# Eight modulation slots of the first block moved from TensorE to VectorE, as sixteen half slots during the projections

## The reference

```python
mod = c @ ada_w[l] + ada_b[l]          # c: 1x1024, ada_w: 1024 x 6144, 24 MB
shift1, scale1, gate1, shift2, scale2, gate2 = jnp.split(mod, 6, axis=-1)
h = _modulate(_rmsnorm(x, norm1_g[l]), shift1, scale1)
z = h @ w_in[l]                        # 256x1024 @ 1024x2720: "the projections"
zu, zv, zr = jnp.split(z, [GMLP_WIDTH, 2 * GMLP_WIDTH], axis=-1)
y_a = _gmlp_mixer(zu, zv, ...)         # gelu, layer norm, mixing by ws, + bs
y_b = _rwkv7_mixer(zr, ...)            # token shift, low-rank gates, a recurrence over tokens
y = jnp.concatenate([y_a, y_b], axis=-1) @ w_out[l]
x = x + gate1[:, None, :] * y
h = _modulate(_rmsnorm(x, norm2_g[l]), shift2, scale2)
y = _hier_moe(h, ...)                  # router, then 32 experts, 6 MB of weights each
x = x + gate2[:, None, :] * y
```

## Times and profile before

| | us |
|---|---|
| median of three runs | 1554.64 |
| lowest, highest | 1552.86, 1556.13 |
| the profiled execution | 1563.66 |
| its span, first to last instruction | 1561.6 |

### The profile page before, as it was taken

One profiled execution on the slowest core, in us unless ns is written; L12 is line 12 of the kernel. 1 busy time (PEld: TensorE's weight loads), 2 busy tenths in 40 slices (PEclk: granted clock), 3 DMA queues, 4 the chain that ended last, 5 costly groups with the idle time before them and its releaser, 6 DMA issues.

```text
span 1561.6 us, 21530 instructions
## 1 busy us (share of the span) xinstructions
PE 1491.0 (95%) x8432; PEld 952.6 (61%) x8433; DVE 463.7 (30%) x835; ACT 233.8 (15%) x469; POOL 22.0 (1%) x69
## 2 busy tenths in 40 slices
PE   6999999999989999999899999999999999999998
PEld 3766775544445444444585657777768564777775
DVE  1355544411111111111453422111144472211112
ACT  1231002300000000000313430000031052100001
POOL 2000000000000000000000000000000000000000
PEclk9999999999999999999999999999999999999999
DMA  9665523899999999999999050444276933144420
GB/s 370 219 258 217 220 110 141 341 404 423 422 417 393 426 426 426 427 427 424 407 402 351 19 222 30 162 162 161 81 264 246 397 116 108 55 162 162 161 81 27
DMA packets 89962, 400.82 MB, mean 257 GB/s; under 512 B 7040, under 2 KB 12288, under 8 KB 63264
## 3 DMA queue, kind: packets, MB, share of 16 engines
q1 hardware_dynamic: 89888, 399.73, 64.6%
HBM read 398.66 MB, written 1.05 MB: 256 GB/s over the span
## 4 chain that ended last, share of the span: by engine, by line
PE 76%; DMA 9%; DVE 7%; issue 3%; DVEq 3%; ACT 1%; SPq 0%; ACTq 0%
PE psum L1358 20%; PE psum L1027 13%; PE psum L1371 10%; DMA ring<-in_moe_up 6%; PE psum L1173 4%; PE psum L637 4%; PE psum L1321 4%; PE psum L1015 2%; DMA arena<-in_w_mod 2%; PE psum L760 2%; PE psum L1206 2%; DMA ring<-in_ada_w 1%; PE psum L566 1%; PE psum L1191 1%; DVE arena L1903 1%
## 5 line engine op out<-in xcount | busy, mean ns | idle before, releaser
L1027 PE MATMUL psum<-ring,arena 128*64 128x256 f32 (+1 forms) x2240 | 306.0, 426 | 18.8 <-DMA ring<-in_moe_up 8.2
L1358 PE MATMUL psum<-arena,ring 128*128 128x256 f32 x1408 | 311.3, 379 | 0.3
L1358 PEld LDWEIGHTS psum<-arena,ring 128*128 128x128 f32 x1408 | 267.1, 190 | 54.3 <-issue 19.8
L1027 PEld LDWEIGHTS psum<-ring,arena 128*64 128x64 f32 x2240 | 162.8, 137 | 170.5 <-issue 77.1
L1371 PE MATMUL psum<-ring,arena 128*128 128x512 f32 x352 | 157.9, 592 | 0.0
L2052 DVE TENSOR_SCALAR arena<-psum,cols 128x256 f32<-128x256 f32 x44 | 23.9, 544 | 323.3 <-PE psum L1358 323.3
L1173 PE MATMUL psum<-arena,ring 128*128 128x256 f32 x512 | 112.2, 380 | 1.5 <-DVE arena L1461 1.5
L1371 PEld LDWEIGHTS psum<-ring,arena 128*128 128x128 f32 x352 | 66.9, 190 | 66.3 <-issue 63.6
L1173 PEld LDWEIGHTS psum<-arena,ring 128*128 128x128 f32 x512 | 96.8, 190 | 16.6 <-issue 3.6
L1816 DVE TENSOR_TENSOR arena<-psum,arena 128x256 f32<-128x256 f32 x32 | 13.6, 425 | 252.1 <-PE psum L1027 252.1
L2392 ACT ACTIVATE arena<-arena 128x256 f32<-128x256 f32 x44 | 18.3, 416 | 415.8 <-DVE arena L2058 415.8
(11 more groups left out here) (383 smaller groups left out, 1238.7 us busy)
## 6 DMA issues: line engine op xcount, KB each, us to landing
ring<-in_moe_gate SPq DMA_DIRECT2D x28, 2048.0 KB, 19.4
ring<-in_moe_up SPq DMA_DIRECT2D x28, 2048.0 KB, 17.8
ring<-in_moe_down SPq DMA_DIRECT2D x28, 2048.0 KB, 18.1
arena<-in_w_mod SPq DMA_DIRECT2D x32, 1024.0 KB, 10.0
ring<-in_ada_w SPq DMA_DIRECT2D x12, 2048.0 KB, 10.4
ring<-in_w_qkv SPq DMA_DIRECT2D x12, 2048.0 KB, 15.0
ring<-in_w_ffn_gate SPq DMA_DIRECT2D x10, 2048.0 KB, 8.0
ring<-in_w_ffn_up SPq DMA_DIRECT2D x10, 2048.0 KB, 12.6
```

The lines of the kernel that those rows point to most:

```text
L1027: ins = mm(bank[b][o, 0:n], lhsT, w[:, half * n:(half + 1) * n], start=first, stop=last, tile_position=(0, 64 * half))
L1358: last = mm(b[:, k * TOK:(k + 1) * TOK], sl[k][2][:, c, j * P:(j + 1) * P], hTd[:, c, :], start=(c == 0), stop=(c == DC - 1))
```

## The change

Slots 4 to 11 of `ada_w` leave TensorE. VectorE does each in two half slots of 128x2048: one multiplication by a column of `c`, added to a running sum (`scalar_tensor_tensor`). Eight half slots make a sum of 128x2048; TensorE then adds its 128 rows up with a vector of ones (`add_slots`, four products) into `part`, and the chain of copy, `flush` and `mod_columns` follows. There are two such sums: `first_sums[0]` in the arena where `bkT` is later, `first_sums[1]` in ring place 0.

On VectorE the sixteen half slots stand as 3 before `shifted(0)`, 1 after it, 2 after `shifted(1)`, 2 after `shifted(3)`, 3 before `shifted(5)`, 3 after the bonus (behind a `mod_columns`), 2 after the gelu's normalization.

On SyncE the loads move up between those of the projections. Ring places come from a table, `FIRST_SLOTS`, for the first 24 loads. A load into a place last held by one of VectorE's slots waits for `mod_step`, which counts half slots. `w_mod0` 2 and 3 are loaded ahead of `w_out`, not after it; the first expert matrix is load 24, as before.

On TensorE the `fill` calls of the Gram products and of level 0 stay and now do `w_mod0` 0 to 3; the other eight slots' worth of `fill` is gone, and two `flush` calls move to the projections and behind the transposes.

```diff
+FIRST_SLOTS = (0, 1, 2, 3, 4, 5, 2, 3, 0, 2, 1, 3, 2, 3, 4, 2, 3, 5, 1, 2, 3, 0, 4, 5)
+OF_VECTOR = (6, 7, 9, 11, 12, 13, 15, 16)
+def last_in(s, n):
+    return max((j for j in range(max(0, n - 4 * RING), n) if slot_of(j) == s), default=None)
+def opened_by(n):
+    return n + 1 - sum(j <= n for j in OF_VECTOR)
...
@@ SyncE
             def load(src, n):
                 s, _, i = st_sp.take()
-                if i >= RING:
-                    sp.wait_ge(S("slot_freed"), i - RING + 1)
+                j = last_in(s, i)
+                if j in OF_VECTOR:
+                    sp.wait_ge(S("mod_step"), 2 * (OF_VECTOR.index(j) + 1))
+                elif j is not None:
+                    sp.wait_ge(S("slot_freed"), opened_by(j))
...
             load(w_cols(a["w_in"], D + HALF), 4096)
+            load_mod("ada_w", 4)
             sp.dma_start(lora[0:64, :], a["lora"]).then_inc(S("lora_in"), 16)
             sp.dma_start(g2s[0:96, :], a["g2"]).then_inc(S("lora_in"), 16)
+            load_mod("ada_w", 5)
             load(w_cols(a["w_in"], D), 4096)
+            load_mod("ada_w", 6)
...
             sp.dma_start(wsT, a["ws"]).then_inc(S("x_in"), 16)
+            for i in range(7, 10):
+                load_mod("ada_w", i)
             load(w_cols(a["w_in"], HALF), 4096)
+            for i in range(10, 12):
+                load_mod("ada_w", i)
             load(w_cols(a["w_in"], 0), 4096)
             sp.wait_ge(S("lora_done"), 6)
...
-            for i in range(4, 12):
-                load_mod("ada_w", i)
-            for i in range(2):
+            for i in range(4):
+                if i == 3:
+                    sp.wait_ge(S("part_done"), 3)
                 load_mod("w_mod0", i)
             for i in range(2):
                 load(w_cols(a["w_out"], 512 * i), 4096)
-            for i in range(2, 4):
-                load_mod("w_mod0", i)
...
@@ TensorE
             features(w, 0)
+            add_slots(8, sums=first_sums[0])
+            filled[0] += 4
             features(w, 1)
...
                 last.then_inc(S("unit_ready"), 1)
+                if t == 0:
+                    flush()
...
+            add_slots(16, sums=first_sums[1])
+            filled[0] += 4
...
                     last.then_inc(S("tok_turned"), 1)
+            flush()
...
-                    if l == 1 - T:
-                        flush()
-                    elif T == 0 and l < 5:
+                    if T == 0 and l == 0:
                         fill(1)
...
-                    if T == 0 and l == 2:
-                        fill(1)
...
             u_of(2)
-            fill(1)
             d_state(2)
-            fill(1)
...
             last.then_inc(S("logits_done"), 1)
-            fill(2)
...
@@ VectorE
+            def mod_halves(n):
+                for _ in range(n):
+                    h = halves[0]
+                    halves[0] += 1
+                    i = OF_VECTOR[h // 2]
+                    dve.wait_ge(S(f"slot{slot_of(i)}_loaded"), 16 * use_of(i))
+                    w = ring[:, slot_of(i), :].rearrange("p (c n) -> p c n", c=2)[:, h % 2, :]
+                    to, by = first_sums[h // 8], col("c1", h % 8)
...
+                        ins = V.scalar_tensor_tensor(out=to, in0=w, scalar=by, in1=to, op0=ALU.mult, op1=ALU.add)
+                    d.to(ins, "mod_step")
+            mod_halves(3)
             shifted(0)
+            mod_halves(1)
             shifted(1)
+            mod_halves(2)
             shifted(2)
...
             shifted(3)
+            mod_halves(2)
             shifted(4)
...
+            mod_halves(3)
             shifted(5)
...
             d(V.tensor_tensor(arT[:, 1], rT, eL, ALU.mult))
+            dve.wait_ge(S("part_done"), 2)
             d(V.tensor_tensor(bkT[:, 0], tmp1, cum, ALU.mult))
...
                                 vT[:, 2 * half:2 * half + 2, :], ALU.mult), "bonus_ready")
+            mod_columns()
+            mod_halves(3)
...
                 d.to(V.tensor_tensor(gv[:, t, :], gv[:, t, :], lnb, ALU.add), "gv_ready")
+            mod_halves(2)
...
@@ ScalarE
             shift(5)
+            part_copy()
             shift(6)
```

More of the change, by code:

```diff
@@ L243, in build_program @@
         macc2 = at(10240, 2 * D)
+        first_sums = (at(17920, 2 * D), ring[:, 0, 0:2 * D])
         mslots = ((at(8192, 2 * D), at(12288, 2 * D)), (at(15360, 2 * D), at(17408, 2 * D)))
@@ L375, in mod_slot @@
                     if j >= 2:
-                        sp.wait_ge(S("mod_step"), 16 * layer + 2 * (j - 1))
+                        sp.wait_ge(S("mod_step"), 16 + 16 * layer + 2 * (j - 1))
                     elif layer == 1:
@@ L541, in take @@
             def take():
+                while st_pe.n in OF_VECTOR:
+                    st_pe.take()
                 s, use, n = st_pe.take()
@@ L619, in fill, with add_slots @@
                     filled[0] += 1
+            def add_slots(steps, start=True, stop=True, sums=macc2):
+                pe.wait_ge(S("mod_step"), steps)
+                if start:
+                    pe.wait_ge(S("mod_copied"), filled[0] // 4)
+                for g in range(4):
+                    last = mm(part[32 * g:32 * g + 1, :], ones[:, 0:1], sums[:, 512 * g:512 * g + 512], start=start, stop=stop,
+                              tile_position=(0, 32 * g))
+                if stop:
+                    last.then_inc(S("part_done"), 1)
             units = [0]
@@ L753, in _, with chunk_products @@
             pe.wait_ge(S("gram_copied"), 16)
-            def chunk_products(out, left, right):
+            def chunk_products(out, left, right, opens=False):
                 for j in range(4):
@@ L761, in chunk_products @@
                                   tile_position=(ps.start, ps.start))
+                        if opens and j == 0 and ps.start == 0:
+                            last.then_inc(S("slot_freed"), 1)
+                            ahead[0] = True
                 return last
@@ L959, in _ @@
             last.then_inc(S("logits_done"), 1)
[L960 removed]
             pe.wait_ge(S("routed"), 6)
             oh = rt[:, 392:456].rearrange("p (t e) -> p t e", t=NT)
[L964 removed]
+            mm(bank[6][:, 0:NE], upper[:, :], oh[:, 0], start=True, stop=True)
             mm(bank[6][:, NE:2 * NE], ones[:, :], oh[:, 0], start=True, stop=False)
@@ L1130, in fill1 @@
                     filled[0] += 1
[L1132 to L1137, removed]
-                    last = mm(part[32 * g:32 * g + 1, :], ones[:, 0:1], macc2[:, 512 * g:512 * g + 512], start=start, stop=stop,
-                              tile_position=(0, 32 * g))
-                if stop:
-                    last.then_inc(S("part_done"), 1)
             def between_units(layer, u):
                 if layer == 0 and u == 2:
-                    add_slots(4, start=False)
+                    add_slots(20, start=False)
                     filled[0] += 2
                 if layer == 0 and u == 7:
-                    add_slots(12)
+                    add_slots(28)
                     filled[0] += 4
                 if layer == 1 and u in (4, 8):
-                    add_slots(16 + 2 * u)
+                    add_slots(32 + 2 * u)
                     filled[0] += 4
@@ L1310, in _ @@
                 if layer == 0:
-                    add_slots(16, stop=False)
+                    add_slots(32, stop=False)
                     filled[0] += 2
@@ L1341, in group_slots @@
                         s = (n + k) % RING
-                        out.append((S(f"slot{s}_loaded"), i * 16 + 16 * ((n + k) // RING + 1),
+                        out.append((S(f"slot{s}_loaded"), i * 16 + 16 * use_of(n + k),
                                     ring[:, s, 0:8 * w].rearrange("p (c n) -> p c n", c=(DC, DC, w // P)[k])))
@@ L1583, in _ @@
                 d.to(V.tensor_copy(tokb[:, t, :], bank[3 + t][:, :]), "tokb_copied")
+            mod_columns()
+            d.to(V.scalar_tensor_tensor(out=modc[:, 0, 32:40], in0=modc[:, 0, 32:40], scalar=1.0, in1=col("norm2_g", 0, 8),
+                                        op0=ALU.add, op1=ALU.mult), "routed")
             dve.wait_ge(S("bonus_ready"), 2)
@@ L2182, in _ @@
                     a_.to(A(dst[:, t, :], bank[1 + 2 * q + t][:, :], ACT.Copy), "tok_copied")
-            for _ in range(2):
-                part_copy()
             nc.scalar.preload_act_table_set("natural_log_exp_and_others")
```

32 lines of the change are left out of this document (20 added, 12 removed).

## The result

| | before | changed |
|---|---|---|
| median of the runs, us | 1555.39 | 1583.68 |
| lowest to highest | 1552.86 to 1556.28 | 1578.61 to 1589.30 |
| profiled execution (span) | 1563.66 (1561.6) | 1589.30 (1587.3) |

The ratio is 1.0176, with a 95% interval of 1.0157 to 1.0194; the medians lie 28.3 us apart. The forecast was +9.9, its range ended at 1571.0. One execution of `e3_both` fell in a slower state of the chip (1930.06 us at a mean granted clock of 0.75) and is left out of its ratio.

The account below looks back on a forecast made before the run. TensorE alone was taken to set the time in the projections, TensorE and VectorE alternately in `inverse(0)`. Lost 19.7 us, gained 9.75: 9.9 slower, from 1554.64 to 1564.5 us, range 1557.0 to 1571.0.

Parts of the forecast that it names:

- before `d_state(2)`: Without the first fill, `d_state(2)` waits only for VectorE's copy, ending at 216.32, not 217.29: 0.9 us gained.
- The last piece of `w_in`: Largest term: before the last projection TensorE idles 8.9 us, as the load queues behind one awaiting the twelfth half slot.
- Rival 3: Load 17 needs no twelfth half slot, the last piece is not late: -1.0, 1553.6 us; chance 0.09, further 0.03 if kinder.
- `shifted(0)`: In the projections, VectorE's third pass waits for `ada_w` 5, so `shifted(0)` is late and `low_rank(0)` waits 2.5 us.
- New work: In the projections and around the transposes, two `add_slots` and their `flush` calls cost TensorE 3.1 us.
- The recurrence: Without fills, levels 1 to 4 of `inverse(0)` gain 8.05 us and a `flush` in `inverse(1)` 0.8: 8.85 us.
- The clock: Half clock after three new gaps, at `low_rank(0)`, the last projection and the routing, costs 1.7, 2.0 and 1.5: 5.2 us.
- The experts: The expert stage moves as a block with TensorE's start; from first gate product to end its length stays the same.
- rival 4: Expert matrices arrive earlier, worth up to two matrices, 9.8 us: sum 0, 1554.7 us; chance 0.04.
- Rival 2: VectorE late as well: D+HALF lands at 36.0, second load takes 14.9, gaps cost 2.8 each: +17.3, 1571.9 us; chance 0.13.

Follow-up runs that it names:

- e3_both: The changed kernel with the last piece of `w_in` ahead of `ada_w` 10 and 11, and two half slots before `shifted(0)`, not three: ratio 1.0049.
- e1_order: The changed kernel with one edit, the last piece of `w_in` loaded ahead of `ada_w` 10 and 11 in SyncE's queue: ratio 1.0087.
- b_again: The kernel before, unchanged, run again for a second trace: 1554.94 us.
- e6_late: `e3_both` with one wait more, so SyncE issues the first expert matrices only after `inverse(0)`: ratio 1.0030.
- e4_idle: The changed kernel plus products without use on TensorE, two behind `d_state(2)` and four in the routing: ratio 1.0133.
- e5_all: `e3_both` plus products without use on TensorE, two before and two behind `d_state(2)`, four in the routing: ratio 1.0021.

## Why the prediction was right in its sign and wrong in its size

Stage by stage, in the changed kernel's trace against that of before (us):

| up to the start of | forecast | measured |
|---|---|---|
| `low_rank(0)` | +2.5 | +4.3 |
| HALF | +2.6 | +5.6 |
| last projection | +10.0 | +11.1 |
| Gram products | +3.1 | +3.6 |
| `inverse(0)` | 0 | 0 |
| `v_terms(0)` | -8.1 | -2.6 |
| `w_out` | -1.7 | +3.5 |
| routing's first product | 0 | 0 |
| first expert | +1.5 | +4.4 |
| end | 0 | -4.2 |

The forecast's terms stand where the prediction has them, the clock's 1.7, 2.0 and 1.5 us in the rows of HALF, the Gram products and the first expert. The largest term came out nearly right. The miss is mostly in what the kernel was to gain between `inverse(0)` and `w_out`, 9.75 us, of which 4.2 are seen in the timelines (2.6 in `inverse(0)`, 0.7 in `inverse(1)`, 0.9 before `d_state(2)`), and in the clock.

**The last piece of `w_in`: right.** The gap was named before the last `features`, with its releaser and the load issued right behind the first pass after `mod_columns`, and all three are in the rows. The size was 10.0 us for 8.9: the piece was used 17.0 us after the flush, for 15.8 forecast, and the load itself took 13.8 for 13.0. `e1_order` shows that nothing else took the gap's place. Rival 3, that the piece is not late, falls by the gap itself.

**`shifted(0)`: right in its mechanism, too small.** `low_rank(0)` waited 6.1 us and started 4.3 later than in the trace of before, for 2.5 forecast. `ada_w` 5 came at 46.5, forecast 44.7. The other part is the baseline: in the trace of before TensorE reached this point at 48.00, in `b_again` at 46.03, since the first projection ran at half clock in the one (3.4 us of 32 to 36, 1.6 lost) and not in the other. The term was reckoned from a late start.

**New work: right.** From the end of the last projection to the Gram products it takes 0.8 us more than before (1.1 forecast), and the first `add_slots` 1.04, the flush 0.95.

**The recurrence: right where it was undisturbed.** Level 1 to level 5 should have taken 16.2 us; `e6_late` shows 16.03. In the changed kernel `inverse(0)` gave only 2.6 of the 8.05 us: 3.2 went into two issue gaps, which the prediction did not have, and 1.6 and 1.5 into half clock at levels 0 and 5, partly the same time. About 0.9 of the 8.05 was the trace's own: its first fill at level 2 took 2.84 us, with issue waits in it, and 1.90 in `b_again`, where the four levels take 23.3 us and not 24.25. Before `d_state(2)` 0.9 was forecast and 0.9 came. The TensorE work that went was eight fills of 1.9 us, 15 us, not some 20; no term hangs on that.

**The clock: the step that failed.** The term was 5.2 us, three gaps at one short price each. Measured were 30.0 us lost, against 13.0 in the trace of before: +17.0, and +26.6 against `b_again`. Of the 15.8 us by which the two spans lie further apart than forecast, the clock is the largest part, 11.8. Three things were wrong with it.

- A gap's price was set at 1.7 to 2.8 us, from two places in the trace where the half level lasted 3.4 and 6.8 us. After the longer gaps, and among small products, the half level lasted longer: 10.2, 10.2, 13.6 and 20.5 us, with 4.6, 2.8, 5.3 and 9.0 us lost.
- The removed fills were priced by the time that TensorE would save: 0.9 us before `d_state(2)`, nothing behind it and in the routing. That they kept the clock up was foreseen for the routing (1.5 forecast, 4.4 measured) but not for the recurrence, where 9.0 us were lost, 6.0 more than in the trace of before, and none forecast. `e4_idle` and `e5_all` show that products without any use do the same service, if they come before the clock has fallen.
- The trace of before was taken for typical. Its own time was 9.0 us above the median, "which I take to stay so", and that was a mistake: of the 13.0 us that it lost at half clock, 9.6 are not lost in `b_again`, which took 1554.94. The changed kernel's profiled execution is 5.6 above its median. So span against span shows +25.7, the medians +28.3.

**The experts: nearly right.** From the first expert's start to the end it takes 1259.8 us in the trace of before, 1259.6 in `b_again` and 1255.6 in the changed kernel. The block moved, and of rival 4 (expert matrices earlier, 9.8 us) nothing is seen: TensorE waits no less for expert matrices than before (14.6 us; 8.2 and 11.4 in the two traces of before). Where 4 us less come from was not tried. But for the last microseconds there is one half-clock stretch behind 331 us (1.7 us lost), for three in the trace of before (5.1), which is 3.4 of the 4.2. TensorE's waits of 0.2 us per expert for VectorE, 6.5 us in all in the trace of before, are in none of the traces with the changed code; the longer waits for matrices stand in their place.

None of the rivals came out. Rival 2 was nearest, with a later `shifted(0)` and dearer gaps, but its sum was 1571.9.

The Trainium skill, page "TensorE: Matmul & The Clock Gate", section "Why this matters for your kernels", had the right warning, and the trace agrees: the projection behind the 10 us wait for a DMA ran at 0.50 until about 137 us and took 2.8 us longer. The prediction drew a price for it from too few rows.

## What to carry to other kernels

Before moving small work off TensorE, ask what the work does for its clock: a filler that hides completely can keep TensorE at full clock, and taking it away can cost more than its length (3.6 us of it in the routing, 4.4 us lost). When loads for a helper engine are put into the one queue that also feeds the critical engine, follow each critical load back to the last semaphore that any load ahead of it waits for; one load put ahead of two others was worth 14 us here. And take a second trace of the baseline before adding up small terms, if the one at hand lies away from its median.

## What was unexpected of the hardware

- The half-clock level could hold for 20.5 us (239 to 260 us) while TensorE was 88% busy by the record, with small products and short waits. In `e5_all`, with 1.98 us of dense products right before `d_state(2)` and as much behind it, it did not come at all. In `e4_idle`, with those behind it alone, it had come before they began; it was broken for some 3.5 us and came back.
- TensorE's waits marked "issue" in the many-product stretch (0.7 and 1.1 us in `e3_both`) were not there in the trace in which no weights were loaded at the same time.
- In the two traces with added products the sum of issue waits among the experts, much later in the program, is 7.3 us (`e4_idle`) and 13.1 us (`e5_all`); in the other eleven it is 1.5 to 4.9. That one has no shown cause.
